# First attention: tiles of a head in the order 7, 0, 4, 5, 2, 6, 3, 1, and the output weights' lo parts one step later

## Chip, cores and metric

One core of one Trainium2 chip. The metric is the device time of one execution in microseconds; lower is better. Engines are called by their names in the profile: PE is TensorE (PEld its weight loads), DVE is VectorE, ACT is ScalarE, POOL is GpSimd, SP is SyncE, which here only issues DMAs.

## What is computed

The reference is a three-layer program on 1024 tokens of width 1024 in float32: one block with a convolution mixer, a pooling mixer, a differential attention and a mixture of experts, then two blocks of another kind. The change lies in the differential attention of the first block and in what follows it at once:

```python
for blk in range(s_len // ATTN_BLOCK):            # 8 tiles of 128 queries
    qb = q[:, :, :, q0:end]; kb = k[:, :, :, :end]; vb = v[:, :, :end]
    s = einsum("bhmqd,bhmkd->bhmqk", qb, kb) * scale     # 4 heads, two maps m each
    s = s - slopes * dist;  s = where(tk <= tq, s, -inf)
    p = softmax(s)
    a = p[:, :, 0] - lam * p[:, :, 1]
    outs.append(einsum("bhqk,bhkd->bhqd", a, vb))
o = rms_norm(concatenate(outs), attn_sub_norm_g) * (1 - lam_init)
mix = concatenate([y_conv, y_pool, o]);  x = x + mix @ w_out
```

The tiles of a head don't depend on each other, so they can be taken in any order. Tile b needs (b+1)*128 key columns.

## The kernel before

The attention is a software pipeline over 32 blocks (4 heads of 8 tiles, list `BLOCKS`, made from `ORDER`). Every engine has its own program, and in each a loop over `g` runs the steps; semaphores tie them together. In step g:

- TensorE computes the scores of block g (line 1774), two maps into banks 0 to 3, after VectorE has read the scores of block g-1 (`s_max`). Then it transposes the combined weights of block g-2 (line 1789), which wait for VectorE's `a_ready`, multiplies those of block g-3 with V (in `accumulate`, line 96), and turns the output of block g-5 back (line 1806).
- VectorE adds the bias and takes the minimum for both maps of block g (line 2315, "CUSTOM_DVE_ANT_0"), then makes the factors of block g-1 (lines 2323, 2324) and combines its two maps (line 2325), and moves the output of block g-5 to `MIX` (line 2331). At a head's first step it also makes the bias row (line 2305).
- ScalarE moves the transposed weights of block g-2 out of PSUM (line 1275), takes the exponentials of both maps of block g (line 1281), and copies and squares the output of block g-3 (lines 1287, 1290).
- GpSimd makes the norm factor of the output and scales it (lines 1027 to 1029).

`TURNS` counts the transposes' groups of at most four 128-column pieces over the blocks, so it follows `ORDER`. In some steps other work is put in: `pooled` (line 1742; two products in each step of `POOLED`) and `pointwise` (in line 96; two in each step of `POINTWISE`). They write banks 1 and 3, which only the scores of tiles 4 to 7 use, so they stand in steps of the tiles 0 to 3, and TensorE waits for ScalarE to empty them before the next scores. SP's loads of x into H wait for the last pointwise product (line 830).

The output weights are used in two parts, a hi part (rounded) and a lo part (the rest). In the last head ScalarE makes the hi part of k-slice n at the end of step NB-NT+n (`o_hi`, line 562), and VectorE subtracts it from the weights in the same step, after its other work (`o_lo`, line 567):

```python
if NB - NT <= g < NB:
    o_lo(dve, 0, g - (NB - NT))
if g in (NB - 1, NB):
    mix1_lo(dve, g - (NB - 1))
```

`mix1_hi` and `mix1_lo` split finished tiles of MIX in the same way; tiles 7 and 0 come first, which is `MIX_ORDER`. After the last step's products TensorE starts the output products (`out_product`, lines 1754 to 1756): the first half of the first one in step NB+2, after `wl_ready` for all eight lo parts and `mx_lo` for tile 7. The two products that begin this stage are of tiles 7 and 0; the third is of tile 1 and waits for every MIX column.

Of the kernel before, what the change touches and what calls it, by code (L numbers as in the profile page):

```python
# [18 lines left out]
NT = S // P  # L19
# [92 lines left out]
def program(nc, A, out):  # L112
    ctx = ExitStack()
    with ctx:
# [121 lines left out]

        LN_SUMS, LN_SQUARES, POOLED, POINTWISE = 2 * NT + 1, 2 * NT + 3, (3, 5), (9, 11)
        B_ORDER = [(3 * c + kind, half) for c in range(2) for kind, half in ((0, 0), (1, 0), (0, 1), (1, 1), (2, 0), (2, 1))]  # L240
        B_DONE = [max(n for n, (v, _) in enumerate(B_ORDER) if v == u) + 1 for u in range(6)]
        K_EARLY = [(0, 1)] + [(n + 1,) for n in range(1, KD - 1)] + [()]

# [1 line left out]

            return 29 + 2 * (n + 1) + (n >= NT + 1) + (n >= NT + 3) + (n >= NT + 5)

        ORDER = [b for i in range(NT // 2) for b in (NT - 1 - i, i)]
        BLOCKS = [(h, b) for h in range(HEADS) for b in ORDER]
        NB = len(BLOCKS)  # L250
        TURNS = [sum(b // 4 + 1 for _, b in BLOCKS[:g]) for g in range(NB + 1)]


        def o_bank(q, at=None):
            return bank(6 + q % 2, P, ((q if at is None else at) % 4) * P)
# [127 lines left out]
        UNITS += [("ga", i, C_GA + i * P, P) for i in range(4)]  # L383
        NU = len(UNITS)
        UI = {(k, i): u for u, (k, i, _, _) in enumerate(UNITS)}

        W_DMAS = [3 if k == "kl" else 1 for k, _, _, _ in UNITS]
# [176 lines left out]
        def part_lo(dve, i, to, of, hi):  # L564

            dve.wait_ge(wh_ready, i + 1)
            dve.tensor_tensor(to, of, hi.bitcast(F32), ALU.subtract).then_inc(wl_ready, 1)
# [39 lines left out]
        def out_hi(n, k):  # L607

            if n == 0:
                return w1_hi[0][k // 4][:, k % 4, :]  # L610
            return w1_hi[1][0][:, k, :] if k < 6 else w1_hi[1][1][:, k - 6, :]
# [8 lines left out]
        def o_lo(dve, n, k):  # L620
            part_lo(dve, W_O + n * KD + k, WTr[:, n, k, :], WT[:, n, k, :], out_hi(n, k))
# [12 lines left out]
        def mix1_lo(dve, i):  # L634
            t = MIX_ORDER[i]
            dve.wait_ge(mx_hi, NT + i + 1)
            ts = slice(t * P, (t + 1) * P)
            dve.tensor_tensor(MIXr[:, :, ts], MIX[:, :, ts], mix1_hi_at(t).bitcast(F32), ALU.subtract).then_inc(mx_lo, 1)
# [1542 lines left out]
        def _(dve):  # L2181
# [118 lines left out]
            for g in range(NB + 5):  # L2300
                if g < NB and g % NT == 0:
                    h = BLOCKS[g][0]
                    if g >= 1:
                        dve.wait_ge(s_max, 2 * g)
                    chain.link(dve.tensor_scalar(BH, shared[:, 0:S], kc[:, K_SLOPE + h:K_SLOPE + h + 1], None, ALU.mult))
                if g < NB:
                    b = BLOCKS[g][1]
                    W = (b + 1) * P
                    for m in range(2):
                        dve.wait_ge(s_ready, g + 1)  # L2310
                        if m == 0 and g >= 3:
                            dve.wait_ge(t_ready, TURNS[g - 2])
                        if m == 1 and g >= 2:
                            dve.wait_ge(a_ready, g - 1)
                        dve.tensor_tensor_reduce(sS[m][g % (3 - m)][:, 0:W], psf[:, 2 * m * HALF:2 * m * HALF + W], BH[:, S - P - b * P:S],
                                                 1.0, -NEG, ALU.add, ALU.min, sm[:, g % 4, m:m + 1]).then_inc(s_max, 1)
                if 1 <= g <= NB:

                    q = g - 1
                    W = (BLOCKS[q][1] + 1) * P  # L2320
                    t = sm[:, q % 4, :]
                    dve.wait_ge(e_ready, 2 * q + 2)
                    chain.link(dve.reciprocal(t[:, 6:8], t[:, 4:6]))
                    chain.link(dve.scalar_tensor_tensor(out=t[:, 7:8], in0=t[:, 7:8], scalar=t[:, 4:5], in1=lam4[:, 4:5], op0=ALU.mult, op1=ALU.mult))
                    dve.scalar_tensor_tensor(out=sS[0][q % 3][:, 0:W], in0=sS[1][q % 2][:, 0:W], scalar=t[:, 7:8], in1=sS[0][q % 3][:, 0:W],
                                             op0=ALU.mult, op1=ALU.add).then_inc(a_ready, 1)
                if g >= 5:
                    q = g - 5
                    h, b = BLOCKS[q]
                    dve.wait_ge(ot_ready, q + 1)  # L2330
                    dve.tensor_scalar(MIX[:, 4 + h, b * P:(b + 1) * P], o_bank(q + 1, q), vec1[:, V_SG:V_SG + 1], None, ALU.mult).then_inc(ot_evac, 1)
                if NB - NT <= g < NB:
                    o_lo(dve, 0, g - (NB - NT))
                if g in (NB - 1, NB):
                    mix1_lo(dve, g - (NB - 1))

# [485 lines left out]
```

## Time and profile before

| | us |
|---|---|
| median of 3 runs | 2321.77 (2321.01 to 2325.1) |
| profiled execution, its own time | 2326.31 |
| its span | 2324.6 |
| PE / DVE / ACT / POOL busy | 2238.0 / 1359.4 / 1074.2 / 512.4 |
| granted TensorE clock, mean over the span | 0.991 |

The first attention runs from about 242 to 376 us of the span, the output products after it to about 479. Busy times are sums over instructions of an engine; TensorE's counts a waiting-free stretch as busy whatever its clock. In the views a row with "<-" in square brackets names what ended the engine's idle time before that instruction. "PEclk" is the share of full speed granted in the stretch.

### The profile page before, as it was taken

To read this page: it belongs to the slowest core of one execution; us is meant where nothing else is said; L and a number is where in the kernel's file an instruction comes from. 1 tells how busy PE (TensorE), PEld (TensorE's weight loads), DVE (VectorE), ACT (ScalarE), POOL (GpSimd) and SP (SyncE) were. 2 spreads that over 40 slices of the span, in tenths; PEclk is the share of its full clock that TensorE was granted. 3 is DMA by queue.
4 is the path that set the end of the run, shared out by engine and by line. 5 is a ranking of instruction groups with operands and counts; after the bars stand their busy time and mean duration, and the time that the engine had idled before them with its cause. 6 is when DMAs were issued, how large, how long until landed. Compare 5 with 4: busy or idle time off the path is not lost.

```text
span 2324.6 us, 30184 instructions
## 1 busy us (share of the span) xinstructions
PE 2238.0 (96%) x11284; PEld 1775.0 (76%) x11284; DVE 1359.4 (58%) x2094; ACT 1074.2 (46%) x1722; POOL 512.4 (22%) x514
## 2 busy tenths in 40 slices
PE   7999888998999999999999999999999999999998
PEld 6877566865666676888878888887788887888886
DVE  5884585345666664576337775345477427776354
ACT  4312775134555556555334444336565344445242
POOL 2167242102233334121220002002212220002001
PEclk9999999999999999999999999999999999999999
DMA  5210210258999974111110013122111110013112
GB/s 131 87 37 1 74 72 11 74 203 323 359 365 346 320 285 167 46 37 28 48 39 23 1 37 145 37 80 86 46 37 37 28 48 23 12 37 136 46 55 100
DMA packets 146491, 236.41 MB, mean 102 GB/s; under 512 B 44096, under 2 KB 100672, under 8 KB 134464
## 3 DMA queue, kind: packets, MB, share of 16 engines
q1 hardware_dynamic: 135136, 209.53, 25.7%
q0 software_dynamic: 8928, 16.80, 3.0%
q10 hardware_dynamic: 2304, 8.39, 0.9%
q8 instruction: 83, 1.36, 0.2%
q14 instruction: 40, 0.33, 0.0%
HBM read 208.98 MB, written 41.42 MB: 108 GB/s over the span
## 4 chain that ended last, share of the span: by engine, by line
PE 71%; DMA 10%; DVE 4%; ACT 3%; issue 3%; POOL 1%; SPq 1%; POOLq 0%; DVEq 0%; ACTq 0%
PE ps L106 13%; PE ps L108 13%; PE ps L107 12%; DMA h_dram<-X 9%; PE ps L96 8%; PE ps L2139 2%; PE ps L1774 1%; PE ps L1754 1%; PE ps L1756 1%; PE ps L1755 1%; PE ps L2092 1%; PE ps L2091 1%; PE ps L2093 1%; PE ps L2130 1%; PE ps L2129 1%
## 5 line engine op out<-in xcount | busy, mean ns | idle before, releaser
L108 PE MATMUL ps<-HT_hi,WF_lo 128*128 128x512 f32 x800 | 312.1, 390 | 0.0
L106 PE MATMUL ps<-HT_hi,WU_hi 128*128 128x512 f32 x704 | 282.5, 401 | 6.3 <-POOL WF_lo L1109 1.9
L107 PE MATMUL ps<-H_lo,WU_hi 128*128 128x512 f32 x704 | 274.1, 389 | 0.0
L107 PE MATMUL ps<-WT_lo,HT_hi 128*128 128x512 f32 x656 | 255.3, 389 | 0.0
L1109 POOL TENSOR_TENSOR WF_lo<-WF,WU_hi 128x1024 fp32r<-128x1024 f32 x42 | 112.6, 2680 | 434.9 <-ACT WU_hi L1392 434.9
L106 PE MATMUL ps<-W_hi,HT_hi 128*128 128x512 f32 x472 | 186.0, 394 | 2.3 <-ACT WF L1667 2.3
L108 PE MATMUL ps<-W_hi,MIX_lo 128*128 128x512 f32 x480 | 187.2, 390 | 0.0
L108 PEld LDWEIGHTS ps<-HT_hi,WF_lo 128*128 128x128 f32 x800 | 150.3, 188 | 32.1
L106 PEld LDWEIGHTS ps<-HT_hi,WU_hi 128*128 128x128 f32 x704 | 132.2, 188 | 39.8 <-issue 3.8
L107 PEld LDWEIGHTS ps<-H_lo,WU_hi 128*128 128x128 f32 x704 | 132.3, 188 | 29.0 <-issue 2.9
L107 PEld LDWEIGHTS ps<-WT_lo,HT_hi 128*128 128x128 f32 x656 | 123.3, 188 | 24.9 <-issue 0.5
L532 POOL TENSOR_SCALAR ss<-ss 128x1 f32<-128x1 f32 x56 | 21.3, 381 | 443.7 <-ACT ps L508 197.6
L1884 PE MATMUL ps<-WT,MIX 128*128 128x512 f32 x248 | 112.3, 595 | 3.5 <-DMA WT<-in_w_up 1.5
L106 PEld LDWEIGHTS ps<-W_hi,HT_hi 128*128 128x128 f32 x472 | 88.7, 188 | 21.2 <-ACT WF L1667 3.2
L2498 DVE TENSOR_TENSOR MIX_lo<-MIX,WK_hi 128x1024 fp32r<-128x1024 f32 x62 | 73.2, 1222 | 54.1 <-ACT WK_hi L1334 54.1
L108 PEld LDWEIGHTS ps<-W_hi,MIX_lo 128*128 128x128 f32 x480 | 90.1, 188 | 19.1
L2739 DVE TENSOR_REDUCE sm<-ps 128x1 f32<-128x1024 f32 x64 | 78.4, 1225 | 44.8 <-PE ps L2130 44.4
L1884 PEld LDWEIGHTS ps<-WT,MIX 128*128 128x128 f32 x248 | 46.3, 189 | 53.5 <-issue 44.5
L2487 DVE TENSOR_TENSOR WT_lo<-WT,WK_hi 128x1024 fp32r<-128x1024 f32 x62 | 73.0, 1218 | 21.6 <-ACT WK_hi L1324 21.4
L1625 ACT ACTIVATE xn<-ps,sm 128x1024 f32<-128x1024 f32 x64 | 71.7, 1120 | 25.5 <-DVE sm L2740 25.5
L1324 ACT ACTIVATE WK_hi<-WT 128x1024 fp32r<-128x1024 f32 x62 | 62.1, 1051 | 39.0 <-DMA WT<-in_w_up 39.0
L2223 DVE SCALAR_TENSOR_TENSOR H<-H,vec 128x1024 f32<-128x1024 f32 x60 | 76.9, 1282 | 1.5
(486 smaller groups left out, 5546.6 us busy)
## 6 DMA issues: line engine op xcount, KB each, us to landing
WT<-in_w_gate SPq DMA_DIRECT2D x31, 1024.0 KB, 7.7
WT<-in_w_up SPq DMA_DIRECT2D x31, 1024.0 KB, 11.4
MIX<-in_w_down SPq DMA_DIRECT2D x31, 1024.0 KB, 11.3
WF<-in_w_in SPq DMA_DIRECT2D x48, 512.0 KB, 3.9
WT<-in_w_out SPq DMA_DIRECT2D x6, 2048.0 KB, 7.9
H<-h_dram SPq DMA_DIRECT2D x24, 512.0 KB, 10.9
H<-in_x SPq DMA_DIRECT2D x16, 512.0 KB, 7.3
h_dram<-H SPq DMA_DIRECT2D x16, 512.0 KB, 3.4
```

Of the source, the lines that this page charges most:

```text
L96: mm = pe.matmul(o, l, r, start=(i == 0), stop=(i == last))
L106: pe.matmul(o, lh, rh, start=(i == 0), stop=False)
L107: pe.matmul(o, lh, rl, start=False, stop=False)
L108: mm = pe.matmul(o, ll, rh, start=False, stop=(i == last))
L1109: pool.tensor_tensor(WFr[:, w, :, 0:n], WF[:, w, :, 0:n], wu_hi[:, w, :, 0:n].bitcast(F32), ALU.subtract).then_inc(ul_ready, 1)
L1324: act.activation(wgu_hi[:, g, :, :], wgu[:, p, g, K0:KD, :], ACT.Copy).then_inc(m_gh, 1)
L1625: act.activation(xn[:, g % 2, :], psf[:, (2 + 2 * (g % 2)) * HALF:(4 + 2 * (g % 2)) * HALF], ACT.Exp, scale=MLA_SCALE, bias=sm[:, g % 2, 1 ...
L1884: pe.matmul(to, hgT[:, p, k, :], wgu[:, p, :, k, :], start=(k == 0), stop=False)
L2223: o = dve.scalar_tensor_tensor(out=y_cv[:, c, :], in0=uu, scalar=w, in1=y_cv[:, c, :], op0=ALU.mult, op1=ALU.add)
L2487: ins = dve.tensor_tensor(wgu_lo[:, p, g, K0:KD, :], wgu[:, p, g, K0:KD, :], wgu_hi[:, g, :, :].bitcast(F32), ALU.subtract)
L2498: ins = dve.tensor_tensor(wd_lo[:, p, k, :], wd[:, p, k, :], down_hi_at(i, o)[:, k, :].bitcast(F32), ALU.subtract)
L2739: hc.link(dve.tensor_reduce(sm[:, g % 2, 0:1], psf[:, (2 + 2 * (g % 2)) * HALF:(4 + 2 * (g % 2)) * HALF], AX.X, ALU.max))
```

## The change

Within each head the tiles are taken in the order 7, 0, 4, 5, 2, 6, 3, 1; before it was 7, 0, 6, 1, 5, 2, 4, 3. The steps with pooled and pointwise products become 4, 7 and 9, 12. VectorE makes the lo part of k-slice n in step NB-NT+n+1, so the last one falls in step NB.

```diff
-        LN_SUMS, LN_SQUARES, POOLED, POINTWISE = 2 * NT + 1, 2 * NT + 3, (3, 5), (9, 11)
+        LN_SUMS, LN_SQUARES, POOLED, POINTWISE = 2 * NT + 1, 2 * NT + 3, (4, 7), (9, 12)
...
-        ORDER = [b for i in range(NT // 2) for b in (NT - 1 - i, i)]
+        ORDER = (7, 0, 4, 5, 2, 6, 3, 1)
...
-                if NB - NT <= g < NB:
-                    o_lo(dve, 0, g - (NB - NT))
+                if NB - NT < g <= NB:
+                    o_lo(dve, 0, g - 1 - (NB - NT))
```

## Rows read from the trace of the kernel before

**Rows 1.** Page, part 1: TensorE's busy time, share of the span, instructions.
```profile
PE 2238.0 (96%) x11284; PEld 1775.0 (76%) x11284; DVE 1359.4 (58%) x2094; ACT 1074.2 (46%) x1722; POOL 512.4 (22%) x514
```

**Rows 2.** Stretches: four heads by first scores, drain, output products; busy times, clock, DMA.
```profile
241.78:270.58 28.80, 24.16 (x135) 14.85 (x135) 19.43 (x55) 20.15 (x55) 5.69 (x11) 0.94 0.40 146
270.58:303.68 33.10, 30.80 (x182) 19.72 (x181) 23.25 (x66) 24.92 (x74) 14.28 (x24) 1.00 0.33 127
303.68:332.47 28.79, 25.82 (x166) 17.90 (x165) 23.24 (x66) 22.26 (x70) 14.27 (x24) 0.94 0.01 2
332.47:361.33 28.86, 21.52 (x146) 14.69 (x145) 24.01 (x62) 23.32 (x68) 11.39 (x22) 1.00 0.00 1
361.33:376.36 15.03, 9.98 (x57) 8.38 (x57) 9.10 (x21) 9.57 (x28) 7.66 (x12) 0.73 0.00 0
376.36:479.00 102.64, 102.64 (x516) 86.79 (x515) 39.14 (x54) 28.62 (x40) 13.95 (x32) 0.99 0.27 81
```

**Rows 3.** Third head, steps from scores to scores: length, TensorE busy, clock, DMA.
```profile
303.68:308.24 4.56, 3.46 (x22) 1.00 0.00 0
308.24:312.12 3.88, 3.25 (x19) 0.74 0.02 6
312.12:316.77 4.65, 4.46 (x27) 0.85 0.00 0
316.77:319.90 3.13, 3.09 (x22) 1.00 0.00 0
319.90:323.41 3.51, 2.81 (x19) 1.00 0.00 0
323.41:326.45 3.04, 3.04 (x21) 1.00 0.00 0
326.45:329.48 3.03, 2.71 (x20) 1.00 0.01 3
329.48:332.47 2.99, 2.99 (x21) 1.00 0.03 5
```

**Rows 4.** Timeline of TensorE: start, length to the modelled end, instruction.
```profile
252.59 1.98 PE L1742 MATMUL ps<-H,small 128*128 128x512 f32 x4
...
275.56 3.70 PE L96 MATMUL ps<-H,xn 128*128 128x512 f32 x8
...
329.48 1.13 PE L1774 MATMUL ps<-X 64*128 64x512 f32 x4 [0.32 <-DVE sm L2315]
...
330.54 0.55 PE L1789 MATMUL ps<-ident,HT 128*128 128x128 f32 x3
...
330.93 1.50 PE L96 MATMUL ps<-WF,HT 128*128 128x128 f32 x12
...
332.47 1.99 PE L1774 MATMUL ps<-X 64*128 64x512 f32 x8
...
346.21 2.02 PE L96 MATMUL ps<-WF,HT 128*128 128x128 f32 x16
```

**Rows 5.** Groups by form, 242 to 375: busy, mean ns, idle before.
```profile
L1029 POOL TENSOR_SCALAR xn<-xn,sm 128x128 f32<-128x128 f32 x30 | 22.0, 735 | 2.9
...
L2315 DVE CUSTOM_DVE_ANT_0 HT<-ps,HT 128x1024 f32<-128x1024 f32 x8 | 9.5, 1222 | 3.8 <-PE ps L1774 2.8 <-DVE HT L2305 1.1
...
L2325 DVE SCALAR_TENSOR_TENSOR HT<-HT,sm 128x1024 f32<-128x1024 f32 x4 | 5.1, 1284 | 0.1
```

**Rows 6.** Waits, 241 to 375: total us, times, longest.
```profile
DVE WT_lo L567 <- ACT W1d_hi L562: 3.0, 4, 1.1
DVE WT_lo L567 <- ACT W1a_hi L562: 2.6, 3, 1.4
```

**Rows 7.** Timeline of the drain.
```profile
366.67 0.77 PE L1789 MATMUL ps<-ident,HT 128*128 128x128 f32 x5 [2.28 <-DVE HT L2325]
...
367.45 0.69 DVE L567 TENSOR_TENSOR WT_lo<-WT,W1d_hi 128x512 fp32r<-128x512 f32 x1 [0.58 <-ACT W1d_hi L562]
...
370.45 1.11 PE L1789 MATMUL ps<-ident,HT 128*128 128x128 f32 x4 [2.24 <-DVE HT L2325]
```

## Prediction, made before the changed kernel was run

> **What bounds the kernel now.** I read the page first, then the stretches of the attention, then its single steps. TensorE is busy for 96% of the span [rows 1], so the question is where it still waits, and whether the edit touches that place. The stretches answer it [rows 2]: from the first scores (241.78) to the first output product (376.36) TensorE works 112.28 of 134.58 us, and from 376.36 to 479 it works without a break (102.64 of 102.64). What is saved before 376.36 therefore arrives at 479 whole, as long as nothing else ends later there.
>
> Inside the attention one score bank set serves all blocks, so the start of block g+1's scores closes step g. I call a block by its width w in 128 columns (tile b has w = b+1). The old order is 8 1 7 2 6 3 5 4, the new one 8 1 5 6 3 7 4 2. Four chains can end a step:
> - A, TensorE's own list: scores of g, transposes of g-2, product of g-3, turn-back of g-5. Starts in the timeline [rows 4] give scores 1.06 for w=4, transposes 0.39 for w=3 and, with the turn-back, 1.54 for the product of w=6. I split that as 1.34 + 0.21, and go by 0.21+0.21w, 0.05+0.11w and 0.22w; for the product of w=8 the timeline has 2.02 [rows 4], for w=7 I take 1.71, between the two.
> - B, scores, then VectorE's two bias-and-minimum passes over them, 1.22 each at w=8 [rows 5]: 4.56 for w=8, 3.51 for w=6, 3.03 for w=5 [rows 3], so about 0.5 a column block: 4.0 for 7, 2.5 for 4, 2.0 for 3.
> - C, the passes of g-1, VectorE's combine of g-2 (1.28 at w=8 [rows 5]), then transposes and product: 0.31 of small operations + (0.14+0.13w) + 0.14 hand-over + transposes + product + 0.21, that is 0.85 + 0.24 w(g-2) + product(g-3), less what step g-1 ran past its B.
> - D, VectorE's own list, where a wide combine stands ahead of narrow passes.
>
> Longest of the chains for the third head, old order, with what was measured [rows 3]: 4.56 B (4.56), 2.92 C (3.88), 3.98 B (4.65), 3.11 C (3.13), 3.51 B (3.51), 3.04 A and C (3.04), 3.03 B (3.03), 2.99 A (2.99); sum 27.14 against 28.79. The two steps that are off, by 0.96 and 0.67, are the two whose granted clock is 0.74 and 0.85. So the chains explain the head, and the clock explains the rest. What a reader should see: the order pairs a wide block's B, in which TensorE idles, with small PE work of narrow blocks behind it.
>
> **The order, a steady head.** New steps by the same chains:
> 8: B 4.56 (A 4.32). 1: C 2.22. 5: B 3.03. 6: A 3.88, because the product of w=8 falls here (B 3.51). 3: D, from the end of the passes of w=6: small operations 0.45, combine of w=5 0.81, move-out 0.26, passes of w=3 about 1.1, less the 0.4 that step 6 ran past its B: about 2.2 (A 1.9, B 2.0). 7: B 3.98. 4: A 2.99. 2: C 3.21 less 0.49 = 2.72. Sum 25.58. Against 27.14 that is -1.6 a head at full clock. The gain is overlap: wide passes now cover wide products (w=7 under the passes of w=8, w=5 and 6 under w=7 and 4). No instruction is added or dropped, and the sums of VectorE's and ScalarE's work are the same.
>
> **Pooled and pointwise products.** They go to steps whose block has w at most 4, as the banks they borrow demand. A pooled pair holds TensorE for about 1.8, a pointwise pair for about 3.5 (1.98 and 3.70 to the last end [rows 4], less the overlap with what follows). Both lie on A before and after. First head: old 28.80 [rows 2]. New: 4.56, 1.11 (only scores and passes yet), 3.4 (D: the combine of w=8 stands ahead of the passes), 3.7 (A without a turn-back), 1.9+1.8, 3.98, 2.99, 2.3+1.8, together 27.5. The old head holds 0.4 of slow clock in its opening (it is at 0.94 [rows 2]), which I leave in: 27.9, so -0.9. Second head: old 33.10 [rows 2]; new 4.56+(1.8+3.5)+3.03+3.88+(1.9+3.5)+3.98+2.99+2.72 = 31.9, so -1.2. Third head: -1.6, from above. The second pointwise pair also releases SP's loads of x into H, now by 1 or 2 us later; their rows are first read after 376, some 80 us on, so that costs nothing.
>
> **The lo parts, last head.** Now VectorE subtracts at the end of step g from a hi part that ScalarE makes last in its own step g, after two exponentials and two copies. It waits 3.0 + 2.6 us for that [rows 6], and the bias passes of the next block stand behind it, and these free the banks for TensorE's next scores. The last head's seven steps to its last scores take 28.86 [rows 2]; the third head's first seven at full clock are 27.14 - 2.99 = 24.15. So hi and lo together cost 4.7. One step later the hi part has long been written: the wait goes, the subtraction of 0.69 [rows 7] stays. In steps 8, 1, 6 and mostly 4 VectorE has that much to spare; in 5, 3 and 7 it hasn't: 0.3 + 0.6 + 0.3, and 0.1 in 4, 1.3 in all. Bounds: 0, if all of it hides, and 7 x 0.61 = 4.3, if none does; 1.3 is nearer the rows, as VectorE works 24.01 of 28.86 there [rows 2]. New: 25.58 - 2.72 + 1.3 = 24.2, so -4.7. The last subtraction is now behind the last step and ends about 2 us ahead of the first output product, which waits for all eight.
>
> **The drain.** From the last scores to the first output product it is 15.03, at a clock of 0.73 [rows 2]; two waits of 2.28 and 2.24 for VectorE's combines stand in it, one with the subtraction of 0.69 and a MIX split ahead of it [rows 7]. A mean of 0.73 is half clock for 0.54 of the stretch, 8.1 us, in which TensorE does about half of its 9.98: 2.4 lost, so 12.6 at full clock. New, with w=4 and w=2 last, down VectorE's list from the last scores: combine of w=7 with its small operations 1.4, move-out 0.3, subtraction 0.6, passes of w=2 0.7, small operations and combine of w=4 1.2: the last transposes but one start 4.2 after. Then move-out 0.3, subtraction 0.6, a MIX split 1.2, small operations and combine of w=2 0.9, and 0.4 until ScalarE has emptied the banks: the last start at 7.6. Transposes 0.3, products 0.9+0.45, turn-backs and their hand-overs 0.9: about 10.2. That is -2.4.
>
> **Sum.** 0.9+1.2+1.6+4.7+2.4 = 10.8 with the slow clock left where it is. That slow clock cost 1.6 in the third head and 2.4 in the drain, and about 1.0 of the first output products, whose stretch is at 0.99 [rows 2, 3]: 5.0 in all. TensorE's idle before 376.36 is 134.58 - 112.28 = 22.3 and falls to about 11.5 with the same work, so part should come back; I take 1.5. Forecast -12.3. The profiled execution took 2326.31 with a span of 2324.6; the median is 2321.77, 4.5 below, which leaves the difference as it is: 2321.8 - 12.3 = 2309.5.
>
> On the clock, what rows show: it is 1.00 in steps where TensorE idles 1.1 of 4.56 us, falls to 0.74 in the step after one of them, and stays 0.73 over the drain with its two long waits [rows 3, 7]. The Trainium skill (TensorE: Matmul & The Clock Gate, HAM oscillation) says that pauses between matmul bursts bring the clock down to half and that each such fall is paid again; with its rule the shorter pauses keep it up, and the time would be the second rival's. The trace agrees for the drain, less plainly for the third head, since the same pause in the second head cost nothing.
>
> GpSimd's scaling of the output takes 735 ns on average for 128 columns [rows 5]. The Trainium skill (SBUF, Who interferes with whom) says that a VectorE instruction with two SBUF inputs and a GpSimd instruction that reads SBUF block one another. The subtraction is such a one. By that rule up to 8 x 0.69 could be added to turn-backs; those have a step of slack here, so the sum would stay.
>
> **Rivals.**
> 1. *VectorE becomes the bound of the last head.* The subtraction is paid in every step: 4.3 instead of 1.3, 2312.5. For it: 24.01 of 28.86 busy. Against: five of eight steps end on TensorE or on scores.
> 2. *The clock stays full.* All 5 come back: -10.8 - 5 = -15.8, 2306.
> 3. *The gain is absorbed later.* Within 0.2%. The third output product needs the last MIX columns, ScalarE's split and VectorE's. It has about 5 us of cover from the products ahead of it, and TensorE never paused there [rows 2]. Or the experts' loads start at a fixed time; nothing in the code ties them to anything but earlier work. 2318 to 2324.
> 4. *Slower: the clock falls in each head.* New pairs 1, 5 and 3, 7 leave TensorE short pauses. One fall in the third head cost 1.6; it decides from (10.8+4.6)/1.6, nine to ten more falls over four heads, where there were two; at 12, 2330. Against: less idle than before.
>
> **How the numbers follow.** The forecast (shorter steps, some clock back) 0.60; rival 1 0.11; rival 2 0.15; rival 3 0.07; rival 4 0.07, half of it mild and so within 0.2% (4.6 us, about what a measurement can tell from no change). Faster 0.86, same 0.10, slower 0.04. Range: from rival 2 with 2 us of spread, 2304, to rival 1 with a clock no better and a fall more, 2317.
>
> **What would show it.** Score starts of the third head: 4.6, 2.2, 3.0, 3.9, 2.2, 4.0, 3.0, 2.7. No wait of the lo subtraction for ScalarE in the last head, and 24 us to its last scores; 10 us of drain. The first output product near 363 to 365. Wrong would be: waits of the scores for VectorE above 1 us in steps 5, 6, 3; a wait in front of the third output product; granted clock under 0.9 in several heads.

## The result, and the profile after

The changed kernel took 2309.32 us (median of 4 executions, 2307.82 to 2310.08) against 2323.43 for the kernel before beside it (4 executions); the ratio is 0.9944, 95% interval 0.9927 to 0.9961. The forecast was 2309.5. In all, 10 executions of the changed kernel (these four and six more) have a median of 2309.16, and 58 others of the kernel before one of 2322.18, which the four beside the first result leave as it is: 13.0 us, 0.56%.

The stretches answer to [rows 2]: four heads from first scores to first scores, the drain to the first output product, the output products (length, then busy time and count of PE, PEld, DVE, ACT, POOL, then clock, DMA share, GB/s).

```profile
241.45:269.62 28.17, 24.34 (x136) 15.10 (x136) 20.09 (x55) 20.45 (x55) 7.54 (x12) 0.94 0.40 148
269.62:301.28 31.66, 30.70 (x181) 19.77 (x181) 22.93 (x65) 25.06 (x74) 12.58 (x24) 1.00 0.30 119
301.28:326.96 25.68, 24.04 (x165) 16.69 (x165) 23.09 (x66) 22.27 (x69) 13.38 (x25) 1.00 0.05 20
326.96:350.96 24.00, 21.71 (x147) 14.86 (x147) 22.78 (x61) 22.57 (x66) 11.48 (x22) 1.00 0.00 1
350.96:361.50 10.54, 6.99 (x54) 5.75 (x54) 9.11 (x22) 9.42 (x30) 6.14 (x11) 1.00 0.00 0
361.50:463.30 101.80, 101.73 (x514) 85.86 (x515) 39.28 (x54) 28.34 (x40) 15.24 (x35) 1.00 0.27 81
```

TensorE does the same work and waits less: 107.78 busy of 120.05 us, 12.3 idle, where it was 112.28 of 134.58, 22.3 idle. Its busy time fell too, by 4.5, although not one instruction went: that is the slow clock of [rows 2], which is gone from the third head and the drain of this profile. The first output product starts at 361.50 instead of 376.36. The output products are as gapless as before, so nothing ends later there.

The steps of the third head answer to [rows 3]: length, TensorE busy, clock, DMA.

```profile
301.28:305.84 4.56, 4.25 (x28) 1.00 0.25 102
305.84:308.21 2.37, 2.01 (x15) 1.00 0.04 10
308.21:311.25 3.04, 2.94 (x23) 1.00 0.00 0
311.25:314.89 3.64, 3.64 (x26) 1.00 0.00 0
314.89:317.22 2.33, 2.02 (x14) 1.00 0.00 0
317.22:321.20 3.98, 3.80 (x25) 1.00 0.00 0
321.20:324.19 2.99, 2.98 (x20) 1.00 0.03 8
324.19:326.96 2.77, 2.40 (x19) 1.00 0.00 0
```

In the first row TensorE is busy for 4.25 of 4.56, where it was 3.46 in the same step before: the product of w=7 now lies under the passes of w=8. That is the overlap that the order buys. The steps of the last head, in which the subtractions stand, in the same columns:

```profile
326.96:331.52 4.56, 4.25 (x28) 1.00 0.00 0
331.52:333.90 2.38, 2.02 (x16) 1.00 0.00 0
333.90:337.06 3.16, 2.94 (x23) 1.00 0.01 3
337.06:340.70 3.64, 3.64 (x26) 1.00 0.00 0
340.70:343.63 2.93, 2.02 (x14) 1.00 0.03 8
343.63:347.90 4.27, 3.81 (x26) 1.00 0.00 0
347.90:350.96 3.06, 3.05 (x20) 1.00 0.00 0
```

Against the head above, step by step: 0, 0, 0.1, 0, 0.6, 0.3, 0.1. Not every step has a subtraction in its way. The first one comes after the passes of w=1, as VectorE's timeline shows (a pass of w=1, the subtraction, a pass of w=5; lines are left out):

```profile
332.71 0.29 DVE L2315 CUSTOM_DVE_ANT_0 HT<-ps,HT 128x128 f32<-128x128 f32 x1
...
334.83 0.69 DVE L567 TENSOR_TENSOR WT_lo<-WT,W1a_hi 128x512 fp32r<-128x512 f32 x1
335.44 0.81 DVE L2315 CUSTOM_DVE_ANT_0 HT<-ps,HT 128x640 f32<-128x640 f32 x1
```

So of the seven steps the five of w=5, 6, 3, 7 and 4 have one ahead of their passes, and the zeros of w=8 and w=1 say nothing of VectorE's room. Of the 0.68 nothing is paid in the step of w=6, which TensorE fills, 0.1 in those of w=5 and 4, 0.3 in that of w=7, and nearly all in that of w=3, where VectorE is the bound. In the view of waits no row "DVE WT_lo <- ACT" is left, where [rows 6] had two. The drain answers to [rows 7] (timeline; lines are left out):

```profile
352.48 0.98 PE L1789 MATMUL ps<-ident,HT 128*128 128x128 f32 x7 [0.82 <-DVE HT L2325]
352.60 0.68 DVE L567 TENSOR_TENSOR WT_lo<-WT,W1d_hi 128x512 fp32r<-128x512 f32 x1
...
355.15 0.66 PE L1789 MATMUL ps<-ident,HT 128*128 128x128 f32 x4 [0.90 <-DVE HT L2325]
...
358.55 0.41 PE L1789 MATMUL ps<-ident,HT 128*128 128x128 f32 x2 [1.07 <-ACT HT L1275]
```

The two waits of 2.28 and 2.24 have become three of about 1, and the last subtraction (358.12) is long done when the first output product needs it.

### The profile page after: what moved, and what is told of

Its sections match the earlier page's. It is cut to its first block, busy times and chain, and to the rows that moved or that the text cites. A ratio compares the mean times of both kernels' runs of the same rounds, so it can differ in the third digit from the quotient of the medians.

```text
span 2306.9 us, 30184 instructions
## 1 busy us (share of the span) xinstructions
PE 2230.6 (97%) x11284; PEld 1770.4 (77%) x11284; DVE 1358.4 (59%) x2094; ACT 1074.1 (47%) x1722; POOL 512.5 (22%) x514
## 4 chain that ended last, share of the span: by engine, by line
PE 71%; DMA 9%; DVE 4%; ACT 3%; issue 3%; POOL 1%; SPq 1%; POOLq 0%; DVEq 0%; ACTq 0%
PE ps L106 13%; PE ps L108 13%; PE ps L107 13%; DMA h_dram<-X 9%; PE ps L96 7%; PE ps L2139 2%; PE ps L1884 1%; PE ps L1754 1%; PE ps L2092 1%; PE ps L2091 1%; PE ps L2093 1%; PE ps L2130 1%; PE ps L2129 1%; PE ps L2127 1%; PE ps L2126 1%
## 5 line engine op out<-in xcount | busy, mean ns | idle before, releaser
L108 PEld LDWEIGHTS ps<-HT_hi,WF_lo 128*128 128x128 f32 x800 | 150.2, 188 | 31.9
L1625 ACT ACTIVATE xn<-ps,sm 128x1024 f32<-128x1024 f32 x64 | 71.7, 1120 | 25.5 <-DVE sm L2740 25.5
L508 ACT ACTIVATE ps<-H 128x1024 f32<-128x1024 f32 x24 | 24.7, 1028 | 114.1 <-DVE H L2765 108.8
```

Of the source, the lines that this page charges most:

```text
L108: mm = pe.matmul(o, ll, rh, start=False, stop=(i == last))
L1625: act.activation(xn[:, g % 2, :], psf[:, (2 + 2 * (g % 2)) * HALF:(4 + 2 * (g % 2)) * HALF], ACT.Exp, scale=MLA_SCALE, bias=sm[:, g % 2, 1 ...
```

## The experiments

e1, e2, e3 and e5 ran on one chip beside 30 executions of the kernel before (median 2322.53); e6, e7, e8 and the changed kernel once more on another beside 17 (2321.19); e9 beside 11 (2322.16) on a third. For each, the stretches are read from the one profiled execution.

**The changed kernel once more.** Six executions, to see whether the first four had been lucky in their clock. Expected before they ran: a mean clock of about 0.994 and a median of 2308 to 2311 if the change takes slow clock away, about 0.992 and 2312 to 2313 if the four were lucky. Measured: 2308.92, mean clock 0.9938. Third head, last head and drain were 25.68, 24.00 and 10.53, as in the first profile.

**e1: the order alone.** The changed kernel with the old place of the subtraction:

```diff
-                if NB - NT < g <= NB:
-                    o_lo(dve, 0, g - 1 - (NB - NT))
+                if NB - NT <= g < NB:
+                    o_lo(dve, 0, g - (NB - NT))
```

> The new order with its pooled and pointwise steps, but the lo parts made in the old step. Theory (chains of the single steps): heads one to three as in the changed kernel (28.2, 31.7, 25.7 us from scores to scores), the last head still waits for ScalarE's hi parts, about 29.5 us to its last scores, and the drain about 11.5; the first output product comes about 5 us sooner than before at full clock, and up to 9 if the slow clock of the drain goes too. Time 2315 to 2319 if the kernel before is 2323. Rival A (the order does it all, by keeping TensorE's clock up): 2311 or less. Rival B (the order does nothing by itself, the lo parts do all): 2322 or more.

Measured: 2316.84 (12 executions), ratio 0.9980 (0.9969 to 0.9991). Its stretches for the third head, the last head and the drain:

```profile
301.83:327.52 25.69, 24.04 (x166) 16.70 (x165) 23.11 (x66) 22.28 (x69) 13.39 (x25) 1.00 0.06 22
327.52:357.20 29.68, 21.91 (x147) 14.85 (x147) 23.70 (x62) 23.23 (x67) 10.92 (x22) 1.00 0.00 1
357.20:368.56 11.36, 6.93 (x53) 5.73 (x54) 8.70 (x21) 9.06 (x28) 6.29 (x11) 1.00 0.00 0
```

and its waits of the subtraction, total, times, longest:

```profile
DVE WT_lo L567 <- ACT W1a_hi L562: 3.3, 3, 1.3
DVE WT_lo L567 <- ACT W1d_hi L562: 2.9, 4, 1.2
```

The third head is that of the changed kernel to 0.01 us; the last is 5.7 longer than there. So the order gives its part in the first three heads without the lo parts. In the last head it gives nothing while the subtraction waits for ScalarE: 29.68 against 28.86 in the kernel before, 0.8 more, with waits of 6.2 in all where [rows 6] had 5.6. Both rivals of this run are out.

**e2: the lo parts alone.** The kernel before with the second part of the change:

```diff
-                if NB - NT <= g < NB:
-                    o_lo(dve, 0, g - (NB - NT))
+                if NB - NT < g <= NB:
+                    o_lo(dve, 0, g - 1 - (NB - NT))
```

> The old order, the lo parts one step later. Theory: heads one to three as before (28.8, 33.1, 27.1 or 28.8 with its slow clock), no wait of the subtraction for ScalarE, last head about 25 us to its last scores instead of 28.9, drain 11.5 at full clock; about 5.4 us off, 2317 to 2318 if before is 2323, and up to 2 or 3 less where the drain loses its slow clock. The parts add up to the whole within 2 us, as they act in different steps: order about 5, lo parts about 5.5, clock the rest. Rival A: 2321 or more. Rival B: 2311 or less.

Measured: 2315.46 (10 executions), ratio 0.9974 (0.9964 to 0.9983). Third head, last head, drain:

```profile
306.16:334.94 28.78, 25.81 (x165) 17.98 (x164) 23.24 (x66) 22.27 (x70) 14.27 (x24) 0.94 0.01 2
334.94:359.48 24.54, 21.24 (x146) 14.71 (x145) 23.11 (x61) 22.34 (x67) 13.29 (x22) 1.00 0.00 1
359.48:370.76 11.28, 7.62 (x57) 6.11 (x57) 9.51 (x22) 9.67 (x28) 5.80 (x11) 1.00 0.00 0
```

The last head's second and third steps (w=1 and w=7) answer a question that [rows 3] left open:

```profile
339.51:342.44 2.93, 2.30 (x19) 1.00 0.00 0
342.44:346.43 3.99, 3.81 (x26) 1.00 0.01 2
```

At full clock they take 2.93 and 3.99, where the prediction's chains gave 2.92 and 3.98 and the third head 3.88 and 4.65: its excess there was the clock.

The last head falls from 28.86 to 24.54, the drain from 15.03 to 11.28 (against 12.54 for the old drain at full clock, e5 below). By the medians the two parts alone give 5.7 and 7.1, together 12.8, and the change 13. The median is 2 us under what the chains alone gave (2317 to 2318); a drain without slow clock fits that, which the expectation had as "up to 2 or 3 less". Both rivals are out.

**e3: the subtraction twice.** Each of the eight is preceded by one like it, whose result goes to a free row and is not used:

```diff
                 if NB - NT < g <= NB:
-                    o_lo(dve, 0, g - 1 - (NB - NT))
+                    k = g - 1 - (NB - NT)
+                    dve.wait_ge(wh_ready, W_O + k + 1)
+                    dve.tensor_tensor(xn[:, 1, 0:HALF], WT[:, 0, k, :], out_hi(0, k).bitcast(F32), ALU.subtract)
+                    o_lo(dve, 0, k)
```

> The changed kernel, with each of the eight lo subtractions of the last head preceded by one more like it, whose result is not used (it goes to a free row buffer). If the one subtraction left costs the head about 1.3 us because most of it hides in VectorE's idle time, a second has less to hide in: 0.6 a step in nearly all steps, last head 27 to 28 us instead of 24.0, drain 1 longer: 3.5 to 5 us slower than the changed kernel, about 2313 to 2314. If VectorE still has room in most steps (it is busy 22.8 of 24.0): under 2 us slower. If VectorE was not the path at all: no change.

Measured: 2314.04 (8 executions), 4.9 over the changed kernel's 2309.16, which ran on other chips. Last head and drain:

```profile
327.57:354.47 26.90, 21.93 (x147) 14.93 (x147) 25.68 (x66) 23.02 (x67) 14.07 (x22) 1.00 0.00 1
354.47:366.71 12.24, 7.44 (x54) 6.23 (x54) 10.82 (x25) 9.06 (x28) 7.92 (x12) 0.94 0.00 1
```

The first subtraction cost 1.1 in the seven steps (the sum of differences above). The second costs 2.9, of 5 x 0.6 = 3.0 that five more subtractions hold: VectorE's idle time, in which the first was hidden, is used up. The drain is 1.7 longer, part of it slow clock (0.94). The steps of w=8 and w=1, with no subtraction ahead of their passes, still stand at 4.57 and 2.37.

**e5: TensorE kept busy in the old drain.** The kernel before with three matmuls, whose result nobody reads, in the two waits:

```diff
+                    if g >= NB:
+                        pe.wait_ge(s_max, 2 * NB)
+                        for _ in range(1 + (g == NB + 1)):
+                            pe.matmul(bank(3), ident[:, :], V1[:, 0, :], start=True, stop=True)
                     pe.wait_ge(a_ready, q + 1)
```

> The kernel before, with three matmuls of 128x512 whose result nobody reads put into TensorE's two waits of the drain (one ahead of the last transposes but one, two ahead of the last), into a bank that is free there. If the slow clock of the drain came from those waits: the granted clock stays 1.00 over the drain and the first output products, the drain takes about 12.6 instead of 15.0, and the time falls by 2 to 3.5 us, to about 2320. If the clock falls anyway, or the added matmuls delay the transposes: no change or up to 1 us slower.

Measured: 2322.07 (11 executions), ratio 0.9998 (0.9986 to 1.0009). The drain of its profiled execution:

```profile
362.27:374.81 12.54, 10.32 (x63) 6.99 (x63) 9.10 (x21) 9.56 (x28) 7.00 (x11) 1.00 0.00 0
```

In the profile it did what was expected: 12.54 at clock 1.00 instead of 15.03 at 0.73, the full-clock drain that the prediction had put at 12.6. That is one profiled execution against one. The time did not follow by the 2 to 3.5 expected. The mean clock over all executions says why that bet was too high: 0.9923 here, 0.9914 over the 30 beside it, a difference of 0.0009. Over the 58 executions of the kernel before, the time falls by 1.35 us for each 0.001 of mean clock (a straight line through them), so 1.2 us is what there was to get; by the means it is 1.0 (2321.25 against 2322.25), which this measurement can't tell from nothing. The profiled execution of [rows 2] was one of the slower ones: 2326.31, where the median is 2322. How often the drain of the kernel before is at the slow clock, and so what filling it is worth, stays open.

**e6 and e7: two other orders.** Both are the changed kernel but for these lines:

```diff
-        ORDER = (7, 0, 4, 5, 2, 6, 3, 1)
+        ORDER = (7, 0, 5, 4, 1, 6, 2, 3)      # e6
+        ORDER = (7, 0, 2, 3, 4, 1, 5, 6)      # e7, with POOLED (2, 5), POINTWISE (9, 11)
```

> The changed kernel with the tiles in the order 7, 0, 5, 4, 1, 6, 2, 3 (widths 8 1 6 5 2 7 3 4), pooled in steps 4 and 7, pointwise in 9 and 12. Worked out with the chains of single steps, the steady head takes 25.3 instead of 25.7, the last 23.4 instead of 24.0, the drain about 11.3 instead of 10.5; first output product 1.1 us sooner in all. Time 0 to 2 us under the changed kernel, not to be told from it. If what counts is only that a wide tile isn't followed by narrow ones (pairs), it could be anything within 5 us; then the step lengths will show it: chains expect 4.5, 2.5, 3.5, 3.7, 2.0, 4.0, 2.5, 2.7.

> The changed kernel with the tiles in the order 7, 0, 2, 3, 4, 1, 5, 6 (widths 8 1 3 4 5 2 6 7), pooled in steps 2 and 5, pointwise in 9 and 11. By the chains a head ends wide, 6 and 7, and 8 follows, so that VectorE's combines of 6 and 7 stand ahead of the passes of 8 and 1: steps of the steady head 4.8, 3.9, 3.7, 3.4, 3.1, 2.5, 3.6, 4.0, together 29.0 instead of 25.7, last seven 25.5, drain 13.9 instead of 10.5. First output product 10 to 11 us later than in the changed kernel: time 2319 to 2324, about that of the kernel before, though the lo parts are late. Rival: the order matters little and the lo parts do most: 2312 or less.

e6: 2308.53 (6 executions), not to be told from the change. Its third head takes 25.27 (expected 25.3), in steps of 4.56, 2.48, 3.52, 3.43, 2.15, 3.99, 2.60, 2.54. Its last head and its drain, expected at 23.4 and 11.3:

```profile
326.12:349.54 23.42, 21.50 (x150) 1.00 0.01 1
349.54:360.75 11.21, 7.49 (x56) 1.00 0.00 0
```

e7: 2323.66 (12 executions), ratio to the kernel before 1.0011 (1.0000 to 1.0022), 14.5 over the changed kernel. Its third head's steps, its last seven steps, its drain:

```profile
303.72:308.44 4.72, 3.35 (x19) 1.00 0.00 0
308.44:312.32 3.88, 2.85 (x24) 1.00 0.01 2
312.32:315.86 3.54, 3.54 (x28) 1.00 0.02 5
315.86:319.08 3.22, 3.22 (x24) 1.00 0.00 0
319.08:322.11 3.03, 2.16 (x16) 1.00 0.00 0
322.11:324.60 2.49, 2.07 (x16) 1.00 0.00 0
324.60:328.11 3.51, 3.26 (x24) 1.00 0.01 2
328.11:332.09 3.98, 3.37 (x21) 1.00 0.01 4
332.09:358.63 26.54, 22.14 (x143) 0.94 0.01 1
358.63:375.77 17.14, 12.51 (x67) 0.72 0.00 0
```

The head is 28.4 where the chains gave 29.0, the largest miss of a step 0.18. The second row shows chain C: after the wide pair 6, 7 a narrow step of w=1 takes 3.88, since VectorE first has to combine the block of w=7. The last seven steps take 26.54 and not 25.5, at a clock of 0.94, and the drain 17.14 and not 13.9, at a clock of 0.72, with waits of 2.00 and 2.08 in it; neither forecast held slow clock. This is the strongest single test of the steps: the order, with its pooled and pointwise steps and the lo parts late in both, moves the kernel by 14.5 us, more than the whole change. Of these some 10 are steps and the rest clock (mean 0.9906 against 0.9940, at the 1.35 us for 0.001 of e5). The rival, 2312 or less, is out.

**e8: five of the eight subtractions on GpSimd.**

```diff
-                if NB - NT < g <= NB:
+                if NB - NT + 5 < g <= NB:
                     o_lo(dve, 0, g - 1 - (NB - NT))
...
                 pool.tensor_scalar(o, o, rsq, None, ALU.mult).then_inc(o_n, 1)
+                k = q - (NB - NT - 2)
+                if 0 <= k < 5:
+                    o_lo(pool, 0, k)
```

> The changed kernel, with the first five of the eight lo subtractions of the last head on GpSimd, after its scaling of an output, and the last three on VectorE as in the change. If the subtraction that is left on VectorE costs the last head what the steps 5, 3 and 7 run over (1.3 us in all), the last head's seven steps take about 23.2 instead of 24.0 and the drain 0.1 to 0.4 more: 0 to 1 us under the changed kernel. If GpSimd's subtraction (about 1.4 us, two inputs in SBUF) blocks VectorE's combines: 2 us or more over it, and single combines longer than 1.28.

Measured: 2307.25 (6 executions), ratio to before 0.9939 (0.9923 to 0.9955). Last head and drain, then GpSimd's groups in both (busy, mean ns, idle before):

```profile
328.97:351.88 22.91, 21.64 (x147) 14.86 (x147) 20.33 (x58) 21.67 (x65) 16.60 (x25) 1.00 0.00 1
351.88:363.23 11.35, 7.17 (x54) 5.81 (x54) 8.97 (x20) 9.97 (x30) 10.37 (x13) 1.00 0.00 0
...
L1029 POOL TENSOR_SCALAR xn<-xn,sm 128x128 f32<-128x128 f32 x14 | 13.4, 956 | 1.4
L567 POOL TENSOR_TENSOR WT_lo<-WT,W1a_hi 128x512 fp32r<-128x512 f32 x4 | 5.9, 1474 | 0.0
```

The last head falls by 1.1, which is just what the subtraction cost there: the five that were moved are the five that stood ahead of the passes, and its steps are again those of the third head, 4.56, 2.37, 3.04, 3.64, 2.33, 3.98, 2.99. No combine of VectorE is longer than 1.28, so the rival of this run is out. The drain becomes 0.8 longer. GpSimd's scaling of the outputs is slower there (956 ns on average from 326 us on, 644 in the same window of the changed kernel), but TensorE's two longest waits in that drain, 1.91 and 1.24, end on ScalarE's copies (L1278), so the cause of the 0.8 isn't shown. Net 0.3 by the profile, 1.9 by the medians, within the noise of 6 executions.

**e9: e6 and e8 together.** The two edits above in one kernel.

> The order of e6 (7, 0, 5, 4, 1, 6, 2, 3) and the first five lo subtractions on GpSimd as in e8. By the chains the first output product comes 1.4 us sooner than in the changed kernel (1.1 by the order alone, 0.4 by GpSimd alone): heads one to three as in e6 (27.3, 30.9, 25.3), last seven steps about 22.9, drain about 11.4. Time 1 to 3 us under the changed kernel's 2309.2, about 2307. If its four executions and six of e6 only differed in their clock: between 2308 and 2310.

Measured: 2308.66 (6 executions), ratio 0.9937 (0.9920 to 0.9954); last seven steps 23.02, drain 11.89. Expected were 22.9 and 11.4. Inconclusive: none of e6, e8 and e9 is told from the changed kernel, and what the steps give is about what the drain takes.

## Why the prediction was right

Point by point, by its own steps:

| term | forecast | measured in the profile |
|---|---|---|
| first head | 27.9 | 28.17 |
| second head | 31.9 | 31.66 |
| third head | 25.6 | 25.68 |
| last head, seven steps | 24.2 | 24.00 |
| drain | 10.2 | 10.54 |
| sum over before, slow clock apart | -10.8 | -10.4 (old drain by e5's 12.54) |
| slow clock given back | -1.5 | about -3, by the executions' mean clocks |

- *The bound and its chains.* They held in the third head of every order that was run at full clock, each step within 0.3. In the changed kernel the steps were 4.56, 2.37, 3.04, 3.64, 2.33, 3.98, 2.99, 2.77 against 4.6, 2.2, 3.0, 3.9, 2.2, 4.0, 3.0, 2.7. The largest miss, 0.24 in the step of w=6, is the product of w=8, taken at 2.02; this step is 3.64 with TensorE busy throughout, so the product takes about 1.8 there. The steps of w=1 and w=3 were 0.15 low. Outside it one step missed by more: the first head's third took 4.19 for 3.4, at a clock of 0.63, of which the 0.4 left in the sum covers half. In the drain VectorE's list came out to the step: the last transposes but one started 4.19 after the last scores (forecast 4.2), the last 7.59 (7.6). The 0.34 too little lies behind them.
- *The lo parts.* The wait is gone (no row), the subtraction that is left costs 1.1 in the seven steps (forecast 1.3), and e3 and e8 show it from both sides: twice, +2.9; off VectorE, -1.1. Two things in the prediction were wrong here and did no harm. It counted a subtraction in each of the seven steps, with room for it in 8 and 1, but only five steps have one ahead of their passes, so the bound was 5 x 0.61 = 3.1 and not 4.3, and rival 1 was priced 1.2 too high. And it put 0.3 on the step of w=5, which cost 0.1. Rival 1 is out at either price. In the new order the late lo parts are worth more than in the old one: 6.5 us of last head and drain (e1: 41.04; change: 34.54) against 5.6 (e5's 12.54 with a last head of 28.85: 41.39; e2: 35.82). That is why the sum of the parts, at full clock, is a little under the whole.
- *The products that were moved* cost what they were forecast at: the pooled steps took 3.69 and 4.09 (3.7, 4.1), the pointwise ones 5.27 and 5.42 (5.3, 5.4).
- *The clock.* Its term was the weak one: 1.5 was chosen between nothing and rival 2's 5.0 and not worked out, and it was too small. The mean granted clock rises from 0.9916 (58 executions before) to 0.9940 (10 after); at 1.35 us for 0.001 that is 3.2 us. At the same mean clock of 0.994 the kernels take 2319.66 (9 executions) and 2309.36 (6): 10.3 apart; moved along that straight line to the same clock, all 58 and all 10 are 9.7 apart. So the 13.0 are about 10 of shorter steps and about 3 of clock. Part of the 3 can be placed. All three profiles with the old order (before, e2, e5) have a slow stretch in the third head, whose mean clock is 0.94, and none of the eight with another order has; it costs 1.6. The drain differs from one profile to another (0.73 before, 0.72 in e7, 0.94 in e3, 1.00 in the others), and with one profile for each kernel but the changed one it can't be said what it adds to the medians. Why the clock falls in just those places is not shown. Less idle time is not the whole of it: the old last head, at 1.00, idles 7.3 of 28.86 us, the old third head, at 0.94, only 3.0 of 28.79.
- *The sum came out at 2309.5* partly because two misses met: I set the median of the kernel before at 2321.8 from three runs, and it is 2322.2, while the steps gave 0.5 less and the clock 1.5 more than said. That these two nearly cancel is luck; either alone would have put the number off by 0.5 to 1.5 us, well inside the range.
- *Rivals 2, 3 and 4.* By the medians rival 2 (2306, all 5 of the slow clock back) came half true; inside the attention it came true in both profiles of the changed kernel, with the third head and the drain at 1.00. Nothing was absorbed: a later point, the start of the routing products, came at 490.11 instead of 505.58, 15.5 sooner in the profiles. No new fall of the clock appeared in the heads. The time that GpSimd's scaling was said to be open to, 8 x 0.69 at most, did not appear either: from the last head's first scores to the first output product it took 650 ns on average, where it was 735 over the attention before.

## What to carry to other kernels

When a hand-ordered pipeline has one buffer set between two engines, write each step's length as the longest of a few chains, check them on the steps that the profile shows at full clock, and then work out other orders on paper: here this told a bad order (e7, forecast 10 to 11 us behind in its steps) from a good one, and each step of the third head to 0.3. Check too which instruction of the queue stands ahead of which: a cost was counted seven times here that stood in five places. Look for in-order queues where a cheap instruction waits for another engine's last instruction of the same step: here the wait for it cost about 0.6 us a step (28.86 to 24.54 over seven steps, e2), and nothing spoke against making it one step later. Before a few microseconds are given to a cause, compare executions at the same mean clock, since one profiled execution can be 4 us from the median. A stretch at the slow clock in a single profile (here the drain) may not be there in the next; one that returns in every profile (the third head) belongs to the kernel.

## What the runs showed of the hardware

- The time of one unchanged kernel ran from 2315 to 2327 us over 58 executions, and followed the mean granted clock: 2326.5 at 0.989 (13 executions), 2321.9 at 0.990 (7), 2322.7 at 0.991 (15), 2319.7 at 0.994 (9), 2316.5 at 0.995 (5). At one value it still varies by 3 or 4 us (2321.6 to 2325.3 at 0.991). I had expected 4 us of spread, from the three times shown.
- The slow clock has its places: in the old order's third head it came in each of three profiles (mean clock 0.94), in their last heads in none (1.00), although in the kernel before the second step of both heads holds the same two waits, 1.10 and 0.63 us.
- GpSimd's subtraction of 128x512 took 1.27 to 1.95 us (five of them, e8) where VectorE's takes 0.68, and GpSimd's scaling in the same stretch 0.96 us on average instead of 0.64. The Trainium skill (SBUF, Who interferes with whom) says that a VectorE instruction with two SBUF inputs and a GpSimd instruction that reads SBUF contend with each other. The two longest scalings of e8 agree: 1.87 and 2.09 us, where the shortest take 0.61, while VectorE subtracts and splits a tile of MIX. VectorE's own instructions kept their lengths (subtraction 0.68, combine of w=8 1.28), and its side gained (last head 22.91 against 24.00).
